# Work at the seams between the stages of a transformer layer, moved in the engines' orders

## The reference, cut to what matters

```python
def rmsnorm(x, g):
    return x * rsqrt(mean(x * x, -1) + 1e-6) * g

h = rmsnorm(x, g_norm_mix)
qa, ka, va, qb, kb, vb = split(h @ w_in)            # 1024 -> 2304 columns
qb, kb = partial_rope(qb), partial_rope(kb)         # first 16 of 64 dims of a head
oa = neighbourhood_attention(qa, ka, va, na_rpb)    # 8 heads, 8 x 16 window, learned bias
ob = windowed_gqa_sink(qb, kb, vb, swa_sink)        # 8 query heads, 2 key heads, |q-k| <= 128
o = concatenate([rmsnorm(oa, g_out_na), rmsnorm(ob, g_out_swa)])
x = x + o @ w_out
h = rmsnorm(x, g_norm_ffn)
x = x + (silu(h @ w_gate) * (h @ w_up)) @ w_down    # 1024 -> 2816 -> 1024
out = rmsnorm(x, g_final)
```

## Time and profile before

| | us |
|---|---|
| median of 3 runs | 2262.09 (2261.32 to 2263.62) |
| the profiled run | 2259.97 |
| its span | 2258.2 |
| PE busy | 2208.8 |
| DVE busy | 1440.5 |
| ACT busy | 922.3 |
| POOL busy | 327.8 |

### The profile page before, as it was taken

The page is one execution under the profiler, slowest core; times in us unless marked ns, Lnnn a source line. Parts: engine busy times, 40 slices in busy tenths (PEclk is TensorE's granted clock), DMA queues, the critical chain, the costliest instruction groups (busy, mean ns, idle before and its releaser), DMA issues.

```text
span 2258.2 us, 33189 instructions
## 1 busy us (share of the span) xinstructions
PE 2208.8 (98%) x11464; PEld 1818.5 (81%) x11464; DVE 1440.5 (64%) x2747; ACT 922.3 (41%) x1824; POOL 327.8 (15%) x304
## 2 busy tenths in 40 slices
PE   7999999999999999999999999999999999999998
PEld 6888888788877788778888887888888877888886
DVE  4412143399899777776666657665656578565776
ACT  4411121288888633343333334433333333131342
POOL 3370001145334100011212120000000002020100
PEclk9999999999999999999999999999999999999999
DMA  6472425789954275675545457323232286353544
GB/s 225 140 186 99 140 87 148 201 217 246 235 143 111 83 226 200 224 265 175 189 165 199 154 209 263 128 80 131 80 131 73 102 305 234 104 177 108 191 145 152
DMA packets 274677, 376.68 MB, mean 167 GB/s; under 512 B 15258, under 2 KB 182306, under 8 KB 269168
## 3 DMA queue, kind: packets, MB, share of 16 engines
q1 hardware_dynamic: 266528, 354.15, 49.3%
q0 software_dynamic: 5568, 11.87, 2.0%
q10 hardware_dynamic: 2448, 8.91, 1.4%
HBM read 237.77 MB, written 140.31 MB: 167 GB/s over the span
## 4 chain that ended last, share of the span: by engine, by line
PE 89%; DVE 6%; DMA 2%; issue 2%; ACT 1%; POOL 0%; DVEq 0%; ACTq 0%; SPq 0%
PE late_psum L2047 11%; PE late_psum L2048 11%; PE late_psum L2049 11%; PE late_psum L2078 6%; PE late_psum L2080 5%; PE late_psum L2079 5%; PE late_psum L1017 4%; PE late_psum L997 4%; PE late_psum L527 3%; PE late_psum L528 3%; PE late_psum L529 3%; PE late_psum L555 3%; PE late_psum L554 3%; PE late_psum L556 3%; PE late_psum L985 2%; PE late_psum L1396 2%
## 5 line engine op out<-in xcount | busy, mean ns | idle before, releaser
L2047 PE MATMUL late_psum<-ff_h,ff_ring 128*128 128x512 f32 x1232 | 479.9, 390 | 5.9 <-DVE ff_acts L1907 3.0
L2049 PE MATMUL late_psum<-ff_h,ff_ring 128*128 128x512 f32 x1232 | 479.3, 389 | 0.0
L2048 PE MATMUL late_psum<-ff_h,ff_ring 128*128 128x512 f32 x1232 | 479.3, 389 | 0.0
L2047 PEld LDWEIGHTS late_psum<-ff_h,ff_ring 128*128 128x128 f32 x1232 | 231.2, 188 | 55.9 <-DVE ff_h L1868 3.9
L2049 PEld LDWEIGHTS late_psum<-ff_h,ff_ring 128*128 128x128 f32 x1232 | 231.2, 188 | 48.1
L2048 PEld LDWEIGHTS late_psum<-ff_h,ff_ring 128*128 128x128 f32 x1232 | 231.2, 188 | 47.7
L2078 PE MATMUL late_psum<-ff_d,ff_a 128*128 128x512 f32 x616 | 240.6, 391 | 8.3 <-DVE ff_x L1967 5.3
L2079 PE MATMUL late_psum<-ff_d,ff_a 128*128 128x512 f32 x616 | 239.7, 389 | 0.0
L2080 PE MATMUL late_psum<-ff_d,ff_a 128*128 128x512 f32 x616 | 239.7, 389 | 0.0
L1967 DVE TENSOR_TENSOR ff_x<-late_psum,ff_x 128x512 f32<-128x512 f32 x224 | 153.6, 689 | 121.4 <-PE late_psum L2080 121.0
L1863 DVE TENSOR_TENSOR ff_ring<-ff_raw,ff_ring 128x512 fp32r<-128x512 f32 x176 | 127.5, 726 | 104.3 <-ACT ff_ring L1740 104.1
(11 more groups left out here) (159 smaller groups left out, 4148.9 us busy)
## 6 DMA issues: line engine op xcount, KB each, us to landing
acts_scratch<-ff_acts SPq DMA_DIRECT2D x22, 1792.0 KB, 7.8
ff_a<-acts_scratch SPq DMA_DIRECT2D x24, 960.0 KB, 5.1
ff_raw<-in_w_gate SPq DMA_DIRECT2D x44, 512.0 KB, 3.8
ff_raw<-in_w_up SPq DMA_DIRECT2D x44, 512.0 KB, 3.9
ff_d<-down_scratch SPq DMA_DIRECT2D x21, 768.0 KB, 6.3
att_q_stack<-qk_scratch SPq DMA_DIRECT2D x56, 256.0 KB, 5.2
ffn_in_scratch<-mix_h_stage SPq DMA_DIRECT2D x8, 1792.0 KB, 6.2
ff_h<-ffn_in_scratch SPq DMA_DIRECT2D x14, 1024.0 KB, 7.6
```

Of the source, the lines that this page charges most:

```text
L2047: pe.matmul(out_bank, whi[:, k], hhi[:, :, k], start=(k == 0 and not onto), stop=False, skip_group_check=onto)
L2048: pe.matmul(out_bank, whi[:, k], hlo[:, :, k], start=False, stop=False, skip_group_check=onto)
L2049: last = pe.matmul(out_bank, wlo[:, k], hhi[:, :, k], start=False, stop=(k == 3), skip_group_check=onto)
```

## The change

Seven edits, in the order of the run.

1. Project to attention: the turn of the last token tile moves on PE from behind score 1 to behind score 3, its hi part on ACT from before the first exp to between exp 4 and exp 5, its lo part on DVE from behind shift 1 to step 5. POOL's bias sums of kind 1 now wait for the last rope (`last_roped`). The first turn waits for one release less, and values of unit 3 wait for the last turn's bank (`last_turn_read`).
2. Mix: `stats(0)` moves on PE from before product(0,1) to behind it.
3. The second early operand of h is split and loaded with tile 12 instead of 11.
4. The loads of ff_h2 to ff_h4 (`load_next_h`) move on SP to before the store of tile 15.
5. First half of h: ACT's casts of ff_h2 to ff_h6 move from beside products 0, 2, 4, 6, 8 to beside 1, 3, 5, 7, 9, DVE's subtractions from the same products to beside 2, 4, 6, 8, 10. POOL's first down sums wait for all seven.
6. Second half: casts beside products 4, 6, 10, 12 of step 10 and 1, 3, 5 of step 11 (before: 8, 10, 12 and 0, 2, 4, 6), subtractions one product later; two loads come behind the weight load of the step.
7. Last sums of activations: from the end of gate and up into the first two rounds of down, two operations each; their store on SP to round 1.

```diff
-        eng.wait_ge(res_lo, QK_STEPS + 2 * NT)
+        eng.wait_ge(res_lo, QK_STEPS + 2 * NT - 1)      # turns_free
+    def last_turn_read(eng):
+        eng.wait_ge(res_lo, QK_STEPS + 2 * NT)
+    def last_roped(eng):
+        eng.wait_ge(roped, 2 * NT)
...
             elif kind == 1:
                 proj.all_read(pool)
+                proj.last_roped(pool)
...
-        stream(act, [(TURN_LAG, copy_turned), (1, set_sinks), (0, exp)],
-               then={UNITS + 1: lambda: mix.o_high(0)})
+        stream(act, [(TURN_LAG, copy_turned), (1, set_sinks), (0, exp)], {4: proj.last_high},
+               {UNITS + 1: lambda: mix.o_high(0)})
...
-               {1: proj.last_low}, {UNITS + NORM_LAG - 1: lambda: mix.o_low(0)})
+               {5: proj.last_low}, {UNITS + NORM_LAG - 1: lambda: mix.o_low(0)})
...
-               {1: proj.last_turn}, {UNITS + TURN_LAG - 1: lambda: mix.product(0, 0)})
+               {3: proj.last_turn}, {UNITS + TURN_LAG - 1: lambda: mix.product(0, 0)})
...
-FIRST_H = (10, 11)
+FIRST_H = (10, 12)
...
+            product(t, 1)
             if t == 0:
                 pe.wait_ge(const_in, 32)
                 stats(0)
-            product(t, 1)
...
             if s == PAIRS - 1:
                 load_h(1, 1)
-                load_h(1, 2)
             if s + 1 < STEPS:
                 load_raw(s + 1, 1)
+            if s == PAIRS - 1:
+                load_h(1, 2)
+                load_h(1, 3)
...
+            if i == 0:
+                pool.wait_ge(h_lo_done, SEVEN)
...
-    H_SPLITS = {(0, 2 * (o - EARLY_H)): (0, o) for o in range(EARLY_H, SEVEN)}
-    H_SPLITS.update({(PAIRS - 1, 8 + 2 * o): (1, o) for o in range(3)})
-    H_SPLITS.update({(PAIRS, 2 * (o - 3)): (1, o) for o in range(3, SEVEN)})
+    H_SPLITS = {n: (0, o) for o, n in zip(range(EARLY_H, SEVEN), (1, 3, 5, 7, 9))}
+    H_SPLITS.update({PER * (PAIRS - 1) + n: (1, o) for o, n in enumerate((4, 6, 10, 12, 15, 17, 19))})
...
-            if (s, at_step) in H_SPLITS:
-                h_lo(*H_SPLITS[(s, at_step)])
+            if n - 1 in H_SPLITS:
+                h_lo(*H_SPLITS[n - 1])
...
-        sums_of_acts(STEPS - 1, 0)
-        sums_of_acts(STEPS - 1, 1)
...
+                if (e, pos) in LAST_SUMS:
+                    sums_of_acts(STEPS - 1, LAST_SUMS.index((e, pos)))
```

More of the change, by code:

```diff
@@ L53 @@
 PAD_R, PAD_C = 23, 63
-Project = namedtuple("Project", "bank_free turns_free all_read near_arrived sync gpsimd scalar vector tensor last_turn last_low")
+Project = namedtuple("Project", "bank_free turns_free all_read near_arrived last_roped last_turn_read sync gpsimd scalar "
+                     "vector tensor last_turn last_high last_low")
 def project_phase(nc, x, g_mix, w_in, rpb, cos2, sin2, ident_in, zeros_in, qk_dram, v_near_dram, v_win_dram,
@@ L401, in scalar @@
                 split_hi(n)
-        turn_tok_hi(3 * NT - 1)
     def turn_lo(t):
@@ L565, in last_turn, with last_high @@
         turn_tok(3 * NT - 1)
+    def last_high():
+        turn_tok_hi(3 * NT - 1)
     def last_low():
         turn_tok_lo(3 * NT - 1)
-    return Project(bank_free, turns_free, all_read, near_arrived, sync, gpsimd, scalar, vector, tensor, last_turn, last_low)
+    return Project(bank_free, turns_free, all_read, near_arrived, last_roped, last_turn_read, sync, gpsimd, scalar, vector,
+                   tensor, last_turn, last_high, last_low)
 class Tiles:
@@ L906, in copy_turned, with scalar @@
         nc.scalar.copy(turned_buffer(kind, u)[:, 0:n], tp[:, u % 2, 0:n]).then_inc(pt_copied, 1)
-    def scalar(mix):
-        stream(act, [(TURN_LAG, copy_turned), (1, set_sinks), (0, exp)],
-               then={UNITS + 1: lambda: mix.o_high(0)})
+    def scalar(proj, mix):
+        stream(act, [(TURN_LAG, copy_turned), (1, set_sinks), (0, exp)], {4: proj.last_high},
+               {UNITS + 1: lambda: mix.o_high(0)})
     def shift(kind, r, u):
@@ L999, in turn, with values @@
         last.then_inc(p_turned, 1)
-    def values(kind, r, u):
+    def values(proj, kind, r, u):
         if u % (4 if kind.near else 2) != (3 if kind.near else 1):
@@ L1007, in values @@
                 pe.wait_ge(v_in[i], 16 * (r + 1) if kind.near else 16 * (NEAR_ROUNDS + 1))
+        if kind.near and u == 3 and isinstance(r, int) and r == 0:
+            proj.last_turn_read(pe)
         pe.wait_ge(pt_copied, PT_BANKS + UNITS * r + u + 1)
@@ L1025, in tensor @@
         pe.sem_inc(pv_done, NEAR_PT_BUFS // 2)
-        stream(pe, [(0, partial(score, proj)), (TURN_LAG, partial(turn, proj)), (PV_LAG, values)],
-               {1: proj.last_turn}, {UNITS + TURN_LAG - 1: lambda: mix.product(0, 0)})
+        stream(pe, [(0, partial(score, proj)), (TURN_LAG, partial(turn, proj)), (PV_LAG, partial(values, proj))],
+               {3: proj.last_turn}, {UNITS + TURN_LAG - 1: lambda: mix.product(0, 0)})
     return Attention(all_scored, all_shifted, weights_split, results_copied, stored, load_first_q, load_first_k, load_first_v,
@@ L1217, in sync @@
                 store_h(t - 1)
+            if t == NT - 1:
+                products_done(sp)
+                feed.load_next_h()
             store_x1(t)
@@ L1432, in down_counts @@
     return {ej: n + 1 for n, ej in enumerate(order)}
-Feed = namedtuple("Feed", "load_raw load_h w_hi w_lo w_sums last_sum h_hi h_lo sync gpsimd scalar vector tensor")
+Feed = namedtuple("Feed", "load_raw load_h load_next_h w_hi w_lo w_sums last_sum h_hi h_lo sync gpsimd scalar vector tensor")
 def feed_phase(nc, w_gate, w_up, w_down, g_final, x1_dram, h_dram, act_dram, down_dram, ff, out, norm_sems):
@@ L1453, in feed_phase @@
     FINAL = ROWS * (len(CHUNKS) - 1)
+    LAST_SUMS = ((0, 6), (1, 2))
     EARLY_H = 2
@@ L1603, in load_x1, with load_next_h, gate_up_sync @@
             .then_inc(x1_in[p], 16)
-    def gate_up_sync(mix):
-        mix.products_done(sp)
+    def load_next_h():
         for o in range(EARLY_H, 5):
             load_h(0, o)
+    def gate_up_sync(mix):
         load_down(0)
@@ L1631, in gate_up_sync @@
             if s == PAIRS - 1:
-                for o in range(3, SEVEN):
+                for o in range(4, SEVEN):
                     load_h(1, o)
@@ L1650, in down_sync @@
         load_a(1, 1)
-        store_acts(STEPS - 1)
         for e in range(LAST + 1):
@@ L1668, in down_sync @@
                 load_a(e + 1, 1)
+            if e == 1:
+                store_acts(STEPS - 1)
             if p == ROWS - 1 and more:
@@ L1793, in gate_up_scalar @@
                 mix.turn_copy(NT - 1)
-            if (s, at_step) in H_SPLITS:
-                h_hi(*H_SPLITS[(s, at_step)])
+            if n in H_SPLITS:
+                h_hi(*H_SPLITS[n])
             if s == STEPS - 1:
@@ L2091, in tensor @@
                     down(e - lag, j)
-    return Feed(load_raw, load_h, w_hi, w_lo, w_sums, last_sum, h_hi, h_lo, sync, gpsimd, scalar, vector, tensor)
+    return Feed(load_raw, load_h, load_next_h, w_hi, w_lo, w_sums, last_sum, h_hi, h_lo, sync, gpsimd, scalar, vector, tensor)
 def rope_tables():
@@ L2205, in _ @@
             proj.scalar()
-            att.scalar(mix)
+            att.scalar(proj, mix)
             mix.scalar()
```

## The result

The changed kernel is slower: 2268.8 us (median of 6 runs, 2264.4 to 2272.5) against 2261.7 for the kernel before (6 runs, 2258.5 to 2263.6). The ratio is 1.0032, 95% interval 1.0021 to 1.0044: 7.2 us slower. The forecast was 2259.7, and its range ended at 2266.5. Forecast and range both missed. The profiled run took 2267.93 us, its span 2266.1.

The account below looks back on a forecast made before the run. PE, busy 98% of the span, bounds the kernel, so only its idle pieces and clock could give time. Terms -3.0 - 3.6 - 1.4 + 6.9 + 3.0 - 1.8 - 2.5 = -2.4: forecast 2259.7 us, 8-in-10 range 2250.5 to 2266.5.

Parts of the forecast that it names:

- First half's splits: Start of gate and up: five late splits of h cost 10.5 us, less old waits that go; +6.9, bounds +3 and +10.
- one fall of the clock: Start of gate and up: the 3.6 us wait at P6 brings half clock once, +3.0 us.
- Middle: Middle of gate and up: no split of h right before L1907, so PE's 2.26 us wait shrinks; -1.8, bounds 0 and -2.3.
- Start of attention: Project to attention: rope undisturbed by POOL's bias sums, first turn at 448 to 448.5; -3.0 us, bounds -4.3 and -1.1.
- The rival: Start of attention does not move, as kind 1's bias comes late for unit 8; term 0, total 2262.7 us; chance .11.
- Second early split: Mix, tile 12: normed tile ready within 0.3 us of PE's need, the 1.70 us wait goes; -1.4, or 0.
- First norm: Mix: product(0,1) fills the wait before the first statistics, some 2.1 us wait at the second; -3.6, bounds -0.6 and -5.8.
- last sums: Seam to down: four sums no longer precede the addition PE waits for; -2.5 us, bounds -3.0 and -0.5.
- The rival of three falls: Waits above two us at P6, P12 and first norm each bring half clock, 3.0 each: 2267.2 us, slower; chance .14.
- The Trainium skill's rule on the shared port pair: Start of attention: each normalise waits up to a whole 1.25 us POOL sum, five cost 4 us; term about -2.

Follow-up runs that it names:

- the run of all gains: Kernel before plus rope wait, statistics behind product(0,1), early splits at tiles 10 and 12 with earlier loads, third second-half operand beside product 13, last sums in down: 2248.71 us, 0.9940.

## Why the prediction was wrong

The forecast's terms add up to -2.4, and the trace ends at +8.0. Of these 10.4 us the middle makes 3.9, the start of attention 3.0, the second early split 1.6 and the rest of down 1.5. The first three are steps of the prediction that failed, the last is a term that it left at nothing. Point by point, as the prediction put it:

- *First half's splits, "+6.9", and one fall of the clock, "+3.0".* Right in the mechanism of the waits and in their sum, 10.5 against 10.0. The clock's 3.0 came out by luck: two errors, in the number of falls and in the cost of one, cancelled. The waits were forecast as 1.7, 3.6, 1.1, 1.1 and 3.0 and came as 1.51, 3.34, 1.29, 0.97 and 2.91. There were two falls in place of one, each of some 1.5 us in place of 3.0: PE's lag grew from 6.2 at 1018.9 to 7.7 four us later. The long one has the chain that was forecast, here on ACT and DVE ahead of 994.87:

```profile
988.85 0.59 ACT L1788 COPY ff_gate<-late_psum 128x512 f32<-128x512 f32 x1 [2.05 <-PE late_psum L2071]
989.46 1.28 ACT L1793 ACT_TABLE_LOAD   x1
990.75 0.63 ACT L1793 ACTIVATE ff_gate<-ff_gate 128x512 f32<-128x512 f32 x1
991.29 0.60 ACT L1762 CAST ff_ring<-ff_sums 128x512 fp32r<-128x512 f32 x1
```

```profile
991.92 0.69 DVE L1885 TENSOR_TENSOR ff_ring<-ff_sums,ff_ring 128x512 fp32r<-128x512 f32 x1 [4.98 <-ACT ff_ring L1762]
992.53 2.28 DVE L1890 TENSOR_TENSOR ff_h<-ff_h 128x2048 fp32r<-128x2048 f32 x1
```

  The prediction took POOL's new wait for a saving ("which the new wait of POOL spares"). Beside the moved splits it is one, 2.4 us in the traces. By itself it costs 4.9 us. The changed kernel's trace shows no wait of PE for it, since PE was late at that place anyhow.
- *Middle, "-1.8".* Failed, in sign: +2.1. The step was "no h_lo stands right before L1907". But the third split still stood there, with only one weight's lo part between it and that operation (L1929 now), and I did not ask whether the load of the one that was moved earlier had landed. Its bound, "0 (loads of h 2 and 3 late behind the weights)", named the wrong loads; it was the load of h 1 that came late. How the 2.81 us divide between the two is open. The runs showed the way that works: move the split behind L1907, not away to the front.
- *Start of attention, "-3.0".* The first turn came even a little before the forecast (447.19, "448 to 448.5"). The step that failed is "The last tile's turn and lo part, put at steps 3 and 5, cost what they cost before". They carry two stores, and the mask load is queued behind these on SP: it was issued at 454.94, 6.2 us later than with the rope wait alone. The rival gave another cause, the bias for unit 8, which was not late; its result, no gain, was what came.
- *Second early split, "-1.4".* Failed: +0.2. The hand count took the operand as landed; ACT waited 3.34 us for it, and PE 2.13. With the load a tile earlier the wait was gone.
- *First norm, "-3.6", last sums, "-2.5".* Right in mechanism and, in these two traces, in size: -3.5 and -2.5, with waits of 1.91 ("2.1") and 1.20 ("about 1") left. But for the norm the size is luck of the clock. Of the nine profiles with the statistics moved, six had half clock behind that wait, and their norm gave 1.9 us in place of 3.5. Of the five with them where they were, two had 6.8 us of half clock there, two 3.4 and one none. The run with these two edits alone gained 3.8 us in time, not the 6.1 of the two terms.
- *The rival of three falls, "2267.2".* It named nearly the right total and one of the three places wrong: not the first norm but the middle. The total is luck, since it took 3.0 for each fall and they cost about 1.5; the rest came from the terms that failed above.
- *The Trainium skill's rule on the shared port pair* ("SBUF — State Buffer") was weighed for normalise: by it each would wait up to a whole sum. The changed kernel's first four took 1.45 and three times 0.89 us (0.41 free; two of them below), and POOL's six 7.79 in place of 7.52. Each of the four ends 0.2 us behind the end of one of POOL's sums (446.73, 448.07, 449.42 and 450.77). So each waited for what was left of one sum, the first for a whole one, as the rule has it. Together that is 2.5 us, the 2.4 that the forecast laid on five and not the 4.

```profile
445.50 1.45 DVE L956 TENSOR_SCALAR att_probs<-att_probs,att_rtotal 128x384 f32<-128x384 f32 x1
...
447.40 0.89 DVE L956 TENSOR_SCALAR att_probs<-att_probs,att_rtotal 128x384 f32<-128x384 f32 x1
```

  The Trainium skill's rule ("SBUF — State Buffer", on who interferes with whom: a vector operation with two inputs in SBUF against a GpSimd one that reads it) fits the pace of 1.7 us of the run with POOL's wait, where I had not applied it. That was the more costly place. (Of the rope rows, which the prediction read as each one sum long, the first took 0.85 us, the other three 1.25 to 1.30.)

Three of the four failed or incomplete steps are one mistake: a step was moved, and what it issues or waits for on a queue was not followed (a landing twice, an issue behind a store once).

Left open: the 1.5 us that were lost in down behind 1840. Runs with down as before lost 1.8 (start of attention alone), 2.0 (rope wait alone), 1.1 (POOL's wait alone) and 0.3 (splits alone) there, and the run with the loads a tile earlier lost 3.9, by its wait at 1898. So the loss is no mark of this change. In the changed kernel most of it, 1.3 us, comes at three places, around 1920, 2020 and 2140, and there POOL splits down weights beside DVE's splits. At the first of them a split on DVE (`ff_a`, 128x768) took 3.67 us against 3.38 before. Why it differs from run to run was not tried.

## What to carry to other kernels

When a step is moved, write down what stands ahead of it in its queue at the new place and when its own load lands, and move the load first; the two casts that were moved ahead of their loads cost more than the waits they were to spare. Cover is counted from the last thing that the step waits for to its first use, in this ring one product, not from its place in the list. A conflict between DVE and POOL is best left where DVE has slack: the wait that took it off one split put it on the sums of weights, behind which PE stood 3.65 us. And a saving that was read off one trace should be set beside a second one of the same kernel, since the clock alone moved the first norm by 1.5 us or more.

## What the runs showed of the hardware

**The same wait brings half clock in one run and not in the next.** The wait of 1.91 us at the second statistics left the clock at 1.00 in the changed kernel (776 to 782 above) and had half clock behind it in the run of all gains, as in five more of the nine profiles that have this wait:

```profile
779.01 0.61 PE L1375 MATMUL late_psum<-mix_ones,mix_squares_summed 128*128 128x2 f32 x4 [1.91 <-DVE mix_squares_summed L1296]
```

```profile
780.00:783.00 3.00, 3.00 (x9) 2.36 (x8) 1.37 (x4) 0.20 (x1) 0.00 (x0) 0.57 0.00 0
```

In the other direction 3.34 us at the second new wait had half clock behind it in the changed kernel, and none with the second half put back. Over the 14 profiles, without the start of attention and the last 25 us: of 26 waits of 1.3 to 1.8 us none was followed by half clock, of 34 of 1.85 to 2.4 us twelve, of 20 above 2.6 seventeen. So the forecast's way of asking whether a wait is longer than one that did it (2.68) was too simple: here half clock was the more frequent the longer the wait, and the length alone does not decide it. What else does was not tested. Most spells lasted 3.4 us and cost about 1.5; the one of over six us behind the first norm in the profile of before, from which I took 3, was a long one. Part of the 2257 to 2266 us over which single runs of one kernel lie may be this; it was not tested.
